# RWKV pairs: the next pair's key products go into the level loop, the split of their weights to ScalarE and VectorE, the turns of a behind the loop

## What is computed

```
def rwkv7_prep(u, mu, w_rkv, ...):
    xr, xw, xk, xv, xa, xg = [u + xx * mu[j] for j in range(6)]
    r = heads(xr @ w_rkv[0]); k = heads(xk @ w_rkv[1]); v = heads(xv @ w_rkv[2])
    kk = l2_normalize(k * k_k)
    for d in range(2):
        logw = -softplus(-heads(w0[d] + tanh(xw @ w1[d]) @ w2[d])) - 0.5
        a = sigmoid(heads(a0[d] + (xa @ a1[d]) @ a2[d]))
        kd = k * (1.0 + (a - 1.0) * k_a)
        dirs.append((exp(-exp(logw)), kd, -kk, kk * a))

def wkv7_scan(S0, r, w, k, v, a, b):
    # S <- S diag(w) + (S a) b^T + v k^T ; y = S r, token by token
```

## Time and profile before

| what | value |
|---|---|
| median of three runs | 2406.75 us |
| the profiled execution | 2404.21 us |
| its span in the profile | 2402.4 us |
| TensorE busy | 2294.2 us (95%) |
| VectorE, ScalarE, GpSimd busy | 1560.0, 1264.5, 231.8 us |
| chain that ended last, TensorE's share | 91% |
| the eight pairs | 850.5 to about 1352 us |

### The profile page before, as it was taken

The page is one execution under the profiler, slowest core; times in us unless marked ns, Lnnn a source line. Parts: engine busy times, 40 slices in busy tenths (PEclk is TensorE's granted clock), DMA queues, the critical chain, the costliest instruction groups (busy, mean ns, idle before and its releaser), DMA issues.

```text
span 2402.4 us, 56559 instructions
## 1 busy us (share of the span) xinstructions
PE 2294.2 (95%) x24506; PEld 1851.0 (77%) x24506; DVE 1560.0 (65%) x1761; ACT 1264.5 (53%) x1400; POOL 231.8 (10%) x222
## 2 busy tenths in 40 slices
PE   8999999999999889888988889999999999999998
PEld 4677676888888466666766778888888888888886
DVE  2544776222233855555555268888888888888898
ACT  3422024222222844444444267777787778787875
POOL 2000552000000041111101130000000000000010
PEclk8999999999999989999999999999999999999999
DMA  7556225333222411111110289999999999999994
GB/s 272 193 210 245 71 88 158 88 105 87 97 97 89 144 58 59 58 58 41 54 46 20 95 321 374 365 385 361 383 361 385 360 384 358 385 363 381 360 390 174
DMA packets 228487, 511.90 MB, mean 213 GB/s; under 512 B 15271, under 2 KB 108223, under 8 KB 228031
## 3 DMA queue, kind: packets, MB, share of 16 engines
q1 hardware_dynamic: 225470, 498.61, 56.9%
q10 hardware_dynamic: 1730, 7.10, 0.8%
q0 software_dynamic: 1152, 4.19, 0.5%
HBM read 492.58 MB, written 17.30 MB: 212 GB/s over the span
## 4 chain that ended last, share of the span: by engine, by line
PE 91%; DVE 3%; issue 3%; ACT 1%; DMA 1%; POOL 0%; SPq 0%; DVEq 0%; ACTq 0%; POOLq 0%
PE bank L1673 26%; PE bank L1703 13%; PE bank L1199 3%; PE bank L1200 3%; PE bank L1201 3%; PE bank L1339 2%; PE bank L1313 2%; PE bank L1076 2%; PE bank L1105 2%; PE bank L1077 2%; PE bank L1078 2%; PE bank L1350 2%; PE bank L1217 2%; PE bank L1216 2%; PE bank L1218 2%
## 5 line engine op out<-in xcount | busy, mean ns | idle before, releaser
L3060 DVE TENSOR_TENSOR w_low<-expert_w,w_high 128x1792 fp32r<-128x1792 f32 (+2 forms) x384 | 771.9, 2024 | 120.7 <-ACT w_high L2213 118.1
L2213 ACT CAST w_high<-expert_w 128x1792 fp32r<-128x1792 f32 (+2 forms) x384 | 652.0, 1701 | 217.0 <-PE bank L1673 144.5
L1673 PE MATMUL bank<-w_high,xg_high 128*128 128x448 f32 x1024 | 294.1, 368 | 4.0 <-DVE xg_low L3050 4.0
L1673 PE MATMUL bank<-w_high,xg_low 128*128 128x448 f32 x1024 | 293.1, 367 | 0.0
L1673 PE MATMUL bank<-w_low,xg_high 128*128 128x448 f32 x1024 | 293.1, 367 | 0.0
L1673 PEld LDWEIGHTS bank<-w_high,xg_high 128*128 128x128 f32 x1024 | 191.6, 189 | 21.3 <-DVE xg_low L3050 4.1
L1673 PEld LDWEIGHTS bank<-w_high,xg_low 128*128 128x128 f32 x1024 | 192.8, 188 | 17.0
L1673 PEld LDWEIGHTS bank<-w_low,xg_high 128*128 128x128 f32 x1024 | 192.9, 188 | 15.8
L1703 PE MATMUL bank<-w_high,hid_high 128*128 128x512 f32 x448 | 175.8, 392 | 0.0
L1703 PE MATMUL bank<-w_high,hid_low 128*128 128x512 f32 x448 | 174.9, 390 | 0.0
L1703 PE MATMUL bank<-w_low,hid_high 128*128 128x512 f32 x448 | 174.7, 390 | 0.0
(11 more groups left out here) (440 smaller groups left out, 4035.1 us busy)
## 6 DMA issues: line engine op xcount, KB each, us to landing
expert_w<-in_moe_w_dram SPq DMA_DIRECT2D x128, 1792.0 KB, 9.2
expert_w<-in_moe_w_dram SPq DMA_DIRECT2D x32, 2048.0 KB, 10.4
arena<-in_mod_w_dram SPq DMA_DIRECT2D x48, 1024.0 KB, 8.2
expert_w<-in_moe_w_dram SPq DMA_DIRECT2D x32, 1536.0 KB, 9.7
arena<-in_ffn_w_dram SPq DMA_DIRECT2D x44, 512.0 KB, 5.0
slot_rows<-arena SPq DMA_DIRECT2D x25, 512.0 KB, 5.4
arena<-in_hy_w_in_dram SPq DMA_DIRECT2D x12, 1024.0 KB, 5.3
arena<-in_rw_w_rkv_dram SPq DMA_DIRECT2D x48, 256.0 KB, 2.7
```

The costliest lines, as they stand in the source:

```text
L1673: last = pe.matmul(bank[b0 + v][:, 0:EH], x[:, k, :], w_[:, kk, v * EH:v * EH + EH], start=(k == 0 and x is XGH and w_ is wh), stop=(k == ...
L2213: act.copy(high_piece(kind, n), piece(kind, ering[q % ERN], n // 2, n % 2))\
L3060: dve.tensor_tensor(piece(kind, low[s], n // 2, n % 2), piece(kind, ering[s], n // 2, n % 2), high_piece(kind, n).bitcast(F32), ALU.subtract)\
```

## The change

- **Key products.** `ahead_keys` stands at the head of each round of the level loop. A round takes two of the eight tiles (lv and lv+4), so six products; they accumulate in bank 7, which VectorE clears ahead of the loop (`keys_cleared`), since no product of the loop may start the bank.
- **Their weights.** ScalarE makes the high part (`weights_high`) and VectorE the low part (`weights_low`), for two tiles per round, into `own_high` and `own_low`; the part for round 0 ScalarE makes at the end of the pair before. GpSimd has `next_digits` no more; its `keys_digits` goes round by round.
- **Turns of a.** They stand behind the loop, after those of b, into banks 2 and 3. The ScalarE copies of a follow those of b.
- **Smaller moves.** `ahead_decay(j, 0)` goes ahead of `ahead_rate`; the key copy by ScalarE goes ahead of the copies of b; the waits for the score copies go into the loop; `bonus_in` is counted in another list. SyncE loads the key weights of the pair after next as soon as the last low part is made, and the others as before behind the gate.

The diff, cut to its core:

```diff
@@ SyncE @@
             for i in range(KT):
-                step(sp, "ahead_products", "gate", i - 1)
+                if i < 2:
+                    step(sp, "ahead_products", ("gate", "keys")[i], (-1, 0)[i])
+                else:
+                    step(sp, "ahead_vectors", f"keys_low_{LOOPED - 1}", i - 1)
...
                 sp.wait_ge(sem("ld_pair"), landed + LD_KEYS)
+                if i:
+                    step(sp, "ahead_products", "gate", i - 1)
@@ TensorE @@
-            def ahead_keys(j, tiles):
-                if tiles[0] == 0:
-                    step(pe, "ahead_pool", "next_digits", j - 1)
-                for k in tiles:
-                    mm(bank[4][:, :], keys_w_high[:, k, :], keys_high[k], start=(k == 0), stop=False)
-                    mm(bank[4][:, :], keys_w_high[:, k, :], keys_low[k], start=False, stop=False)
-                    last = mm(bank[4][:, :], keys_w_low[:, k, :], keys_high[k], start=False, stop=(k == KT - 1))
+            def ahead_keys(i, lv):
+                if i == 0:
+                    pe.wait_ge(sem("digits"), lv * 4 + 4)
+                step(pe, "pair_vectors", "keys_cleared", i)
+                pe.wait_ge(sem("ahead_vectors"), key_weights_low(i + 1, lv))
+                settle(pe)
+                for n in range(2):
+                    tokens, rest = (v[n][:, bass.ds(lv * T, T)] for v in (keys_high_part, keys_low_part))
+                    for w, x in ((own_high, tokens), (own_high, rest), (own_low, tokens)):
+                        mm(bank[7][:, :], w[:, n, :], x, start=False, stop=True, skip_group_check=True)
...
-                step(pe, "ahead_copies", "gate", i)
-                for d in range(2):
-                    turn(6 + d, At[d]).then_inc(sem("pair_products"), one("pair_products", f"a_turned_{d}"))
-                for h in range(2):
-                    step(pe, "pair_copies", f"score_copy_{h}", i)
-                settle(pe)
                 with pe.Fori(0, LOOPED) as lv:
+                    if more:
+                        ahead_keys(i, lv)
                     for h in range(2):
-                        level_first(h, lv * 2 + (PER_PAIR * i + h + 1))
+                        level_first(h, lv * 2 + (PER_PAIR * i + h + 1), i)
...
+                for d in range(2):
+                    turn(2 + d, At[d]).then_inc(sem("pair_products"), one("pair_products", f"a_turned_{d}"))
+                step(pe, "ahead_copies", "gate", i)
                 for d in range(2):
+                    if d and more:
+                        step(pe, "ahead_copies", "key_copy", i + 1)
                     turn(6 + d, Kt[d]).then_inc(sem("pair_products"), one("pair_products", f"k_turned_{d}"))
...
                 if more:
-                    ahead_keys(i + 1, range(KT))
                     ahead_rate(i + 1)
-                    ahead_decay(i + 1)
+                    ahead_decay(i + 1, 1)
@@ ScalarE @@
                 for lv in range(LOOPED):
-                    for h in range(2):
-                        first_copy(lv, h)
+                    first_copy(lv, 0)
+                    if more and lv < LOOPED - 1:
+                        weights_high(lv + 1).then_inc(sem("ahead_copies"), one("ahead_copies", f"keys_high_{lv + 1}"))
+                    first_copy(lv, 1)
+                if more:
+                    ahead_keys(i + 1)
                 for d in range(2):
                     step(act, "pair_products", f"b_turned_{d}", i)
                     act.copy(Btok[d], b4(4 + d)).then_inc(sem("pair_copies"), one("pair_copies", f"b_copy_{d}"))
+                for d in range(2):
+                    step(act, "pair_products", f"a_turned_{d}", i)
+                    act.copy(Q[:, d::2, :, 0:C], bank[2 + d][:, :].rearrange("p (b h c) -> p h b c", h=2, c=C))\
+                        .then_inc(sem("pair_copies"), one("pair_copies", f"a_copy_{d}"))
@@ VectorE @@
+            def weights_low(j, lv):
+                dve.tensor_tensor(own_low, wst[:, 1, lv::LOOPED, :], own_high.bitcast(F32), ALU.subtract)\
+                    .then_inc(sem("ahead_vectors"), one("ahead_vectors", f"keys_low_{lv}"))
...
+                if more:
+                    step(dve, "ahead_copies", "query_copy", i)
+                    dve.memset(bank[7][:, :], 0.0).then_inc(sem("pair_vectors"), one("pair_vectors", "keys_cleared"))
+                    step(dve, "ahead_copies", "next_high_0", i)
+                    weights_low(i + 1, 0)
...
                 for lv in range(1, LOOPED + 1):
+                    if more and lv < LOOPED:
+                        step(dve, "ahead_copies", f"keys_high_{lv}", i + 1)
+                        weights_low(i + 1, lv)
                     for h in range(2):
                         join(lv, h)
@@ GpSimd @@
-                if more:
-                    pool.wait_ge(sem("level_turned"), PER_PAIR * (i + 1))
-                    next_digits(i)
```

More of the change, by code:

```diff
@@ L518, in build, with two_parts @@
         wst = sb(3, KT, P)
-        keys_w_low = split("keys_w_low", ut_at + KT * P, KT, P)
-        keys_w_high = split("keys_w_high", (ARENA - D) // 8 * 8, KT, P)
-        keys_high, keys_low = by_tile("keys_high", xt_at), by_tile("keys_low", x_at)
+        own_high = split("own_high", (ARENA - D) // 8 * 8, 2, P)
+        own_low = split("own_low", (ARENA - D) // 8 * 8 + 2 * P, 2, P)
+        def two_parts(name, first):
+            part = LOOPED * T
+            return [split(f"{name}{n}", first + part * n, 1, part)[:, 0, :] for n in range(KT // LOOPED)]
+        keys_high_part, keys_low_part = two_parts("keys_high", xt_at), two_parts("keys_low", x_at)
+        keys_high, keys_low = ([v[k // LOOPED][:, k % LOOPED * T:k % LOOPED * T + T] for k in range(KT)]
+                               for v in (keys_high_part, keys_low_part))
         w2s, a2s, g2a, g2b = sb(P), sb(P), sb(P), sb(P)
@@ L1259, in _, with turn, turn_first @@
             mm = pe.matmul
-            def turn(b, src):
-                for t in range(NB):
+            def turn(b, src, rest=0):
+                for t in range(int(rest), NB):
                     last = pe.transpose(bank[b][:, t * P:(t + 1) * P], src[:, t * P:(t + 1) * P], ident)
                 return last
+            def turn_first(b, src):
+                return pe.transpose(bank[b][:, 0:P], src[:, 0:P], ident)
             def first_keys(k):
@@ L1331, in ahead_gate, with level_first @@
                     .then_inc(sem("ahead_products"), one("ahead_products", "gate"))
-            def level_first(h, count):
+            def level_first(h, count, i):
                 pe.wait_ge(sem("level_ready"), count)
+                step(pe, "pair_copies", f"score_copy_{h}", i)
                 settle(pe)
@@ L2063, in ahead_values @@
                 step(act, "ahead_products", "values", j)
-                act.copy(Vf, bank[6][:, :]).then_inc(sem("ahead_copies"), one("ahead_copies", "value_copy"))
+                done = one("ahead_copies", "value_copy")
+                if j == KT - 1:
+                    done += one("ahead_copies", "next_high_0")
+                act.copy(Vf, bank[6][:, :]).then_inc(sem("ahead_copies"), done)
             def ahead_queries(j):
@@ L2089, in pair @@
                         .then_inc(sem("pair_copies"), one("pair_copies", f"score_copy_{h}"))
-                for d in range(2):
-                    step(act, "pair_products", f"a_turned_{d}", i)
-                    act.copy(Q[:, d::2, :, 0:C], bank[6 + d][:, :].rearrange("p (b h c) -> p h b c", h=2, c=C))\
-                        .then_inc(sem("pair_copies"), one("pair_copies", f"a_copy_{d}"))
                 for lv in range(LOOPED):
-                    for h in range(2):
-                        first_copy(lv, h)
+                    first_copy(lv, 0)
[4 more added lines that the diff above has]
+                    ahead_keys(i + 1)
                 for d in range(2):
@@ L2153, in _ @@
             ahead_values(0)
+            next_high(0)
             ahead_queries(0)
```

101 lines of the change are left out of this document (56 added, 45 removed).

## The result

The changed kernel took 2415.84 us (median of seven runs, 2411.54 to 2421.42) against 2404.18 us of the kernel before (seven runs on the same chip, 2402.79 to 2407.95): a ratio of 1.0048, 95% interval 1.0033 to 1.0062, so some 11.6 us or 0.5% slower. The profiled execution of after, 2420.81 us, lies at the upper end of its runs, that of before at the lower end of its own.

A forecast was written before the change was run, and what follows sets the result against it. TensorE was taken to bound the stage, with idle time from code fetched in blocks. Terms -41.0 + 0 + 28.0 + 7.8 + 4.9 + 4.0 = +3.7 us, taken as +3 on 2406.75, gave 2410 us; range 2395 to 2421.

The forecast's parts named there:

- the likeliest case: Whole kernel: the author's own summed forecast, 2410 us, with a range of 2403 to 2417 us and a chance of 0.47.
- What bounds the stage: Seven pairs: TensorE bounds them, busy 57 to 59 of 62 to 71 us; code-fetch gaps in L1350 total 17.4 us.
- Removed behind z: Behind z: 24 key products of 5.86 us leave each of seven pairs, -41.0 us.
- Round 0: Scores to round 0's end: code-block interval absorbs six added products and removed turns; 0, bounds 0 and +1.46 us.
- round 0 isn't absorbed: Slower rival: round 0's six products stand on the path, 1.46 us x 7 = +10 us, 2420 us; chance 0.23.
- Code blocks: Shifted 256-instruction boundaries: +3 us ahead of round 0's end, +1 us behind the loop; together +4, bounds -4 and +8.
- Turns and ScalarE's queue: Behind the loop: turns of a +7.8 us over eight pairs, longer waits for ScalarE +4.9 us over seven.
- Rounds 1 to 3: Level loop: 18 added key products less covered waits, plus the low clock; +4.0 us a pair, +28.0 us in seven.
- The clock: Behind round 0's stall: 0.50 for 3.4 us, slowing round 1's six key products, +1.46 us less 0.7 on level products.
- The faster rival: Rounds 1 to 3: clock stays up or misses the key products, +2.0 us a pair; 2398 us, chance 0.27.
- The loop fetched anew: Slower rival: the larger loop body no longer stays, each round stalls 4.2 us, +88 us, 2495 us; chance 0.03.

The follow-up runs named there:

- The shift of 75 instructions: Kernel before with 75 one-time instructions without work on TensorE ahead of the RWKV stage, moving the code's block boundaries; 2403.80 us, ratio 1.0007.
- the turns alone: Kernel before with only the turns of a and their copies moved behind the level loop, key products staying behind z; 2406.91 us, ratio 1.0011.
- the last experiment: Changed kernel with key products in the middle of each round, into bank 2, and both turns of a ahead of the loop; 2402.06 us, 0.9994 of kernel before.

## Why the prediction was right in its range and too low in its size

The range, 2395 to 2421, holds the 2415.84 us, and so does the likeliest case's own range up to 2417. The time is 5.8 us over the forecast, and the verdict, slower by over 0.2%, had a chance of 0.35, while "within 0.2%" had 0.37. The loss itself was put far too low: 11.6 us against the 3 of the forecast. That the time still lies in the range is in part luck. The kernel before came out 2.6 us lower in the result than in the median on which the change was laid, and the failed step below lies 14.5 us beyond its own upper bound of 31. Step by step:

- **What bounds the stage** was right: TensorE, with idle time that belongs to its code. The stall in round 0 stayed in each of seven pairs (15.9 us in L1372, 17.4 in L1350 before).
- **Removed behind z**: -41.0 forecast, -39.2 measured from z's end to `wu`, with ScalarE's wait already in it. Right.
- **Round 0** at 0: right in its sum. The stretch takes 9.92 and 10.19 us in pairs 3 and 4, and 11.44 in pair 7, where it may not be absorbed whole. The rival "round 0 isn't absorbed" had a time that fits the result (2413 to 2424), but not its mechanism: it wanted more than 11 us in the pairs with one stall, and two of the three had less. That its range fits shows little, since the cause lies elsewhere.
- **Code blocks**: long pairs 1, 2, 5 and 6 forecast, with some 13.5 us; 14.12, 12.46, 14.18 and 13.16 measured. +3.9 us in this stretch and z together against +4. The shift of 75 instructions shows that the code's place decides which pairs pay. The Trainium skill's "mostly hidden" (Runtime: NRT & Kernel Launch, "Instruction fetch mechanics") isn't borne out by the trace for small products, where these stalls are 15.9 us in L1372 alone.
- **Turns and ScalarE's queue**: +7.8 and +4.9 forecast, of which about 9.3 us ahead of z in seven pairs; 8.2 measured there, 1.3 in the last pair. The wait for ScalarE is the 0.32 us of L1397 (forecast 0.35). Right, and the turns alone gave +7.1. Behind z the sum is about right, but not its reason. The rates start 0.69 us behind z's end, where 1.2 was named and 6.14 before, so 0.41 us more than the 5.86 removed leave. ScalarE's last z copy ends 0.63 us behind z (958.13 + 0.59 against 958.09), as before and not at 1.1: its queue isn't late there. The key products had covered that copy, and now nothing does.
- **Rounds 1 to 3** is the step that failed: +28 forecast (bounds 19 and 31), +45.5 measured. Its first term was 0.97 us of waits that the key products were to cover, most of it put down to VectorE's join by L2879's name. The branch back took as long beside it. The products stand behind the branch, cover the join, and the branch stays, made longer by two register instructions. Idle time was to fall by 6.8 us in seven pairs and rose by 5.9: 12.7 of the 17.5 us. The other 4.8 are busy time: six key products take 1.59 us (940.30 to 941.89) and not 1.46, since the first takes 0.34 us to the second where the others take 0.23, and the low clock covers more (below).
- **The clock**: that the key products of round 1 would run at half clock was right (0.42 us from start to start behind 934.00, 0.23 at full clock). Six of them take 2.85 us (933.41 to 936.26). That the low stretch would stay at 3.4 us was not right:

```profile
932.20:938.90 6.70, 6.22 (x248) 5.06 (x251) 1.53 (x4) 1.05 (x3) 0.00 (x0) 0.52 0.19 54
```

In the second pair the granted clock, 0.50 for 3.4 us before, is 0.52 on average for 6.7 us, from the stall through most of round 1; the `level_second` that starts at 938.00 still takes 1.75 us. Over the seven pairs the low time grew from 47.8 to 56.8 us. Round 1 costs 6.9 - 4.9 = 2.0 us more than round 2.
- **The faster rival** (the clock stays up, the keys fill more than VectorE's waits) fell on both counts. With the keys in the middle of a round its half about the clock came true for rounds 1 to 3. Its price was also too high by 0.7 us a pair: the +2.7 us from which it starts has the 0.7 us of level products at full speed in it already (3.4 - 0.7), and it takes them off again.
- **The loop fetched anew** didn't happen: no stall in rounds 1 to 3, and 65 packets of the instruction queue instead of 69.

That medians differ by 11.6 us and the profiled executions by 16.6 has no cause shown here; executions of the changed kernel differ by up to 10 us. The stretches are read from one execution of each kernel, and add up to 5 us more than the medians show.

Left open: what of the 0.4 us at the loop's head, beside the 0.215 us of the branch itself, could be had back. A loop with fewer waits at its head wasn't tried. Nor is it shown what the 0.29 us are (1.59 - 1.30) that a round with the key products in its middle spends ahead of them.

## What to carry to other kernels

Before work is put at the head of a loop to cover a wait there, look at what the waiting engine's own sequencer does in that time: where the branch back takes as long as the wait, work that stands behind the branch doesn't cover it. Idle time that comes from code not yet there takes in only part of the work that is put into it (1.5 of 5.9 us where a pair had one such stall), and the clock can fall behind it: so ask which operations will stand in the few microseconds behind such a stall, since large products there cost nearly double (2.85 us for six, not 1.59). A move that gains in the stage's idle time and one that loses behind it should be timed apart, as the turns were: the change's loss was the sum of two.

## What the runs showed of the hardware

- TensorE's branch back in the level loop takes 0.207 to 0.231 us in its sequencer in the ten kernels. The gap between the last product of a round and the first of the next is mostly 0.31 to 0.43 us where `level_first` stands at the head, mostly 0.41 us with key products of fixed columns there, and 0.56 us on average (0.39 to 0.78) with columns computed from the loop's counter.
- Seventy-five instructions that run once moved the long stretches, 2.8 to 3.4 us longer than the others, from pairs 4 and 7 to pairs 3 and 6.
- After the stall of round 0 (1.3 us in the third pair with the keys in mid-round, 2.0 us in the second pair of the kernel before) the clock fell to half for 3.4 us or about twice that. With pauses of 0.29 to 0.45 us in the same stretch it stayed at 1.00. The length of one stall doesn't decide it alone: in the last experiment one of 2.11 us (to 1112.26) was followed by no fall, and one of 1.98 us (to 1117.42) by 3.4 us at half.
